# The first norm of a two-block kernel: the roots spread ahead of the last transposes and read in PSUM, the first scaled tile by itself, the first value products begun on the high part

## The chip, the cores and the metric

The kernel runs on one core of one Trainium2 chip. The core has TensorE (PE, matmuls; its weight loads are listed as PEld), VectorE (DVE), ScalarE (ACT), GpSimd (POOL) and SyncE (SP), which issues most DMAs. Each engine works through its own instructions in order and meets the others at semaphores. The metric is the device time of one launch in microseconds, as the median of several runs; lower is better.

## The reference

Two blocks, one after the other, on 512 tokens with 16 meta tokens ahead of them and a width of 1,024, all in fp32. The first block:

```python
h = jnp.concatenate([meta, x], axis=1)                 # 528 positions x 1024
z = rmsnorm(h, norm1_g[l])                             # h * rsqrt(mean(h*h) + EPS) * g
proj = z @ w_in[l]
q, fl, iv, og, pin, ga, gb = jnp.split(proj, SPLITS, axis=-1)
o_a = hgrn2_mixer(q, fl + b_f[l], iv, og, lb_all[l], head_norm_g[l])   # gated linear recurrence, 8 heads
o_b = pool_mixer(pin, w_pool[l], pool_scale[l])
mix = sigmoid(ga) * (o_a @ w_branch_a[l]) + sigmoid(gb) * (o_b @ w_branch_b[l])
h = h + mix @ w_out[l]
z = rmsnorm(h, norm2_g[l])
u, v = jnp.split(z @ w_up[l], 2, axis=-1)
h = h + (silu(causal_dwconv(u, conv_w[l], conv_b[l])) * v) @ w_down[l]
h = rmsnorm(h, final_norm_g)[:, N_META:]
```

The second block projects its norm again, runs two attentions (a latent one with rotary positions and one with forget gates), gates and mixes them, and adds a normed residual. `lb_all` is a softmax over the rows of `lb_logits`; `iv` are the values of the recurrence. Only the head of the first block, up to the first products of `z @ w_in`, is touched here.

## The kernel before

**Products in three terms.** Features lie on the 128 partitions, positions along the free dimension. The state hT is 8 tiles of 128 features x 528 positions; so is z. Each fp32 factor is split into a high part of the faster type fp32r and a rest of the same type: zhi, zlo for the activations, whi, wlo for the weights. A product is the sum of zhi x whi, zlo x whi and zhi x wlo, so a tile of 128 outputs over 8 tiles of features is 8 x 3 matmuls on each of two halves of 264 positions, 48 in all (line 841 is all of them). ScalarE writes the high parts (a copy that rounds), VectorE the low parts (a subtraction). This holds for weights too: a unit of weights (256 columns over 8 feature tiles, 128 x 2048) lands in one of three buffers, ScalarE writes whi (`w_high`), VectorE wlo (`w_low`), and TensorE waits for the latter. The first two units hold the value columns, 4 feature tiles each, so they are half as large.

**Accumulators.** PSUM is 8 banks of 512 fp32 columns. Products accumulate in slots of two banks; slot 0 is banks 0 and 1, slot 1 banks 2 and 3, slot 2 banks 4 and 5. A plan written ahead of the program gives each output tile its slot. The value tiles ("v", 0) and ("v", 1) have slots 0 and 1, computed as a pair, feature tile by feature tile. All later tiles of this stretch alternate between slots 0 and 1. Semaphore `pe_mark` counts finished pieces, `acc_free` the slots that were read out.

**The head.** SP loads the meta tokens (xm) and x (xt) with tokens on the partitions. TensorE transposes them into PSUM, six of eight feature tiles as the token blocks land (banks 0 to 5), the last two after banks 6 and 7 are read out. These transposes are copied to hT: tiles 0 to 3 by VectorE (`h_out` there), 4 to 7 by ScalarE. ScalarE squares x as it lands, one sum a token, then takes logarithm and exponential: the roots, one a token (`rs_ready`). They must be spread over all partitions: VectorE multiplies the identity by them (diag), and TensorE multiplies a matrix of ones by diag, two matmuls of 264 columns into banks 0 and 1 (`rb_spread`); ScalarE copies them to rb in SBUF. Then VectorE writes zt = hT x gain x rb (`norm_zt`, line 1838), ScalarE zhi from it (`norm_hi`), VectorE zlo (`norm_lo`, line 1844); there are two zt buffers. Between these stand the first weight units' parts, in an order written out by hand, as is everything in this kernel: no scheduler decides.

**Behind the value products.** TensorE transposes the small parameter rows (`turn_rows`, in the middle of the value products) and the value tiles (`turn_values`, lines 906 and 908, into banks 5 and 4). The first transposes of value tile 0 wait for ScalarE's copy of it (E<-PS 128x528); then come the q products. On ScalarE, between the last zhi and that copy, stand the high part of unit 2 and a small exponential that waits for VectorE's operations on `lb_logits` (`lb_sub`); between the copies of value tiles 0 and 1 stands the high part of unit 3.

## Time and profile before

| | us |
|---|---|
| three runs | 1569.93, 1570.18, 1575.18 |
| median | 1570.18 |
| profiled execution | 1573.95 |
| its span, first to last instruction | 1572.2 |
| TensorE busy | 1534.9 (98%) |
| VectorE busy | 839.7 (53%) |
| ScalarE busy | 694.7 (44%) |
| DMA, mean | 80 GB/s |

The rows further down come from the one profiled execution. A timeline row gives start and duration of a run of like instructions (x4: four of them), and in brackets the idle time before it and who ended it. A wait is put down to the last releaser. Matmul times are modelled at their ends, so spacing is read from windows: busy time over count. PEclk, the granted share of TensorE's clock, is 1.00 for 2.4 GHz and 0.50 for 1.2 GHz.

### The profile page before, as it was taken

The page shows a single profiled execution, that of the slowest core. Times are in us where ns is not written, and L with a number is a line of the kernel's source. Part 1 is how long each engine was busy: PE and PEld are TensorE (multiplying, and loading weights), DVE is VectorE, ACT ScalarE, POOL GpSimd, SP SyncE. Part 2 cuts the span into 40 slices and gives each one's busy share as a digit, 9 for nine tenths or more (in the row PEclk, how much of TensorE's full clock was granted, in tenths as well). Part 3 has the DMA queues.
Part 4 walks back from the last instruction along what each step waited for, and adds up shares of the span by engine and source line. Part 5 has one row for each costly group of instructions (what it writes and reads, how often), then busy time and mean ns, then how long its engine had stood idle before and what let it go on. Part 6 is the DMA issues. An engine that isn't in the chain of part 4 may idle for free.

```text
span 1572.2 us, 24005 instructions
## 1 busy us (share of the span) xinstructions
PE 1534.9 (98%) x10287; PEld 1350.5 (86%) x10287; DVE 839.7 (53%) x1234; ACT 694.7 (44%) x1036; POOL 3.6 (0%) x16
## 2 busy tenths in 40 slices
PE   7999999999999999999999899999999999999998
PEld 7999999999999989997888777778889877878888
DVE  6477766645645656563334676643233565653343
ACT  5565676654333223232233455542222666653232
POOL 0000000000000000000000000000000000000000
PEclk9999999999999999999999999999999999999999
DMA  6212111214323222232333300113232111122322
GB/s 228 81 55 88 54 55 56 67 31 147 108 81 97 91 92 97 84 105 75 100 94 101 54 1 28 55 54 107 80 108 81 55 54 55 54 68 81 107 81 81
DMA packets 130542, 125.46 MB, mean 80 GB/s; under 512 B 20170, under 2 KB 128485, under 8 KB 130053
## 3 DMA queue, kind: packets, MB, share of 16 engines
q1 hardware_dynamic: 129956, 120.36, 24.2%
q0 software_dynamic: 464, 3.56, 0.6%
q8 instruction: 82, 1.34, 0.4%
q14 instruction: 24, 0.19, 0.0%
q10 hardware_dynamic: 16, 0.00, 0.0%
HBM read 119.66 MB, written 4.26 MB: 79 GB/s over the span
## 4 chain that ended last, share of the span: by engine, by line
PE 89%; DVE 5%; ACT 3%; issue 2%; DMA 1%; DVEq 0%; SPq 0%; ACTq 0%
PE PS L841 75%; PE PS L953 3%; PE PS L1167 2%; PE PS L1110 2%; PE PS L1132 2%; DVE wlo L1798 1%; ACT whi L1307 1%; PE PS L1115 1%; PE PS L1116 1%; DMA raw<-in_w_out 0%; PE PS L1144 0%; PE PS L1117 0%; PE PS L965 0%; DMA xt<-in_x 0%; PE PS L1001 0%
## 5 line engine op out<-in xcount | busy, mean ns | idle before, releaser
L841 PE MATMUL PS<-zhi,whi 128*128 128x258 f32 (+2 forms) x1872 | 486.5, 320 | 6.6 <-DVE zlo L1844 3.3
L841 PE MATMUL PS<-zlo,whi 128*128 128x258 f32 (+2 forms) x1872 | 474.7, 313 | 0.0
L841 PE MATMUL PS<-zhi,wlo 128*128 128x258 f32 (+2 forms) x1872 | 474.4, 313 | 0.0
L841 PEld LDWEIGHTS PS<-zhi,whi 128*128 128x128 f32 x1872 | 308.5, 190 | 31.4 <-issue 9.3
L841 PEld LDWEIGHTS PS<-zhi,wlo 128*128 128x128 f32 x1872 | 307.2, 189 | 21.3
L841 PEld LDWEIGHTS PS<-zlo,whi 128*128 128x128 f32 x1872 | 307.3, 189 | 18.7
L1798 DVE TENSOR_TENSOR wlo<-raw,whi 128x2048 fp32r<-128x2048 f32 (+2 forms) x114 | 247.7, 2173 | 131.2 <-ACT whi L1307 131.1
L1307 ACT ACTIVATE whi<-raw 128x2048 fp32r<-128x2048 f32 (+2 forms) x114 | 207.3, 1819 | 155.6 <-DMA raw<-in_w_up 55.0
L1307 ACT ACTIVATE Pm<-PS,small 128x144 f32<-128x144 f32 (+3 forms) x128 | 68.7, 539 | 60.8 <-DVE small L2315 60.5
L2315 DVE TENSOR_REDUCE small<-PS 128x1 f32<-128x144 f32 (+3 forms) x128 | 63.3, 504 | 45.9 <-PE PS L1117 44.6
L841 PE MATMUL PS<-ghi,whi 128*128 128x512 f32 x176 | 70.3, 399 | 2.2 <-DVE glo L2210 2.2
L841 PE MATMUL PS<-ghi,wlo 128*128 128x512 f32 x176 | 70.2, 399 | 0.0
L841 PE MATMUL PS<-glo,whi 128*128 128x512 f32 x176 | 70.1, 398 | 0.0
L1307 ACT ACTIVATE nsq<-PS 128x512 f32<-128x512 f32 x32 | 19.1, 595 | 102.6 <-PE PS L841 101.2
L1307 ACT ACTIVATE E<-E 128x1056 f32<-128x1056 f32 (+2 forms) x32 | 33.6, 1049 | 52.5 <-DVE E L1942 33.7
L1132 PE MATMUL PS<-ident,Pm 128*128 128x128 f32 x320 | 53.7, 273 | 1.5 <-ACT Pm L1307 0.7
L953 PE MATMUL PS<-E 128*128 128x64 f32 (+1 forms) x448 | 51.8, 268 | 0.7 <-DVE E L1954 0.7
L1307 ACT ACT_TABLE_LOAD x37 | 47.5, 1283 | 7.7 <-PE PS L841 7.1
L841 PE MATMUL PS<-yhi,whi 128*128 128x512 f32 x128 | 50.5, 395 | 0.0
L841 PE MATMUL PS<-yhi,wlo 128*128 128x512 f32 x128 | 50.5, 394 | 0.0
L841 PE MATMUL PS<-ylo,whi 128*128 128x512 f32 x128 | 50.5, 394 | 0.0
L953 PEld LDWEIGHTS PS<-E 128*128 128x128 f32 (+1 forms) x448 | 48.8, 184 | 1.9 <-DVE E L1954 0.9
(351 smaller groups left out, 2150.7 us busy)
## 6 DMA issues: line engine op xcount, KB each, us to landing
raw<-in_w_in SPq DMA_DIRECT2D x50, 1024.0 KB, 5.1
raw<-in_w_up SPq DMA_DIRECT2D x22, 1024.0 KB, 5.1
raw<-in_w_out SPq DMA_DIRECT2D x8, 1024.0 KB, 5.2
raw<-in_w_down SPq DMA_DIRECT2D x8, 1024.0 KB, 5.1
raw<-in_w_br_mla SPq DMA_DIRECT2D x4, 1024.0 KB, 5.1
raw<-in_w_br_fox SPq DMA_DIRECT2D x4, 1024.0 KB, 5.0
raw<-in_w_down SPq DMA_DIRECT2D x4, 768.0 KB, 4.6
hspill<-hT SPq DMA_DIRECT2D x1, 2112.0 KB, 8.3
```

The lines of the kernel that those rows point to most:

```text
L841: ins = mm(o_, l_, r_, start=first, stop=last)
L953: ins = mm(PS[0:m, bank, 64 * it:64 * it + 64].rearrange("p (n b) -> p n b", b=half), e[:, hh, t0:t0 + m], rhs, start=True, stop=True)
L1110: mm(dst, qh[h % 2][:, t0:t0 + P], kh[h % 2][:, c0:c1], start=True, stop=True)
L1115: mm(dst, xqa[i_][:, t0:t0 + P], xka[i_][:, c0:c1], start=True, stop=False)
L1116: mm(dst, xqb[i_][:, t0:t0 + P], xkb[i_][:, c0:c1], start=False, stop=True)
L1132: ins = tr(PS[:, 2 + g % 2, P * x:P * (x + 1)], Pm[h % 2][:, o_:o_ + P], ident[:, :])
L1167: ins = mm(PS[64 * r:64 * r + 64, 7, q0:q0 + n], vtok[0:rows, j, v0:v0 + DV], PT[r][0:rows, c0:c0 + n], start=j == 0, stop=j == 4, skip_gr ...
L1307: return nc.scalar.activation(out_, in_, func, **kw)
L1798: V.tensor_tensor(lo[s_][:, 0:n_], raw[s_][:, 0:n_], hi[s_][:, 0:n_].bitcast(F32), ALU.subtract)\
L2315: V.tensor_reduce(negmax[:, s:s + 1], s_view(i), AX.XY if i == 3 else AX.X, ALU.max, negate=True).then_inc(A.m_ready, 1)
```

## The change

It does four things. (1) The roots' matmuls stand ahead of the last eight transposes, into banks 6 and 7, and the diagonal is built after one hT copy of VectorE's, not two; the last two feature tiles are transposed into banks 0 and 1. (2) No rb: VectorE reads the roots in PSUM when it scales (`root_gain`). (3) The first scaled tile is made by itself ahead of the first low weight part; the second low weight part stands one tile later; ScalarE copies hT tiles 2 and 3, ahead of its first high weight part, and VectorE only tiles 0 and 1. (4) In the value products the two terms with zhi come first, then the one with zlo, each with its own wait (`values_pair`). Since banks 0 and 1 are in use, the value tiles are in slots 1 and 2, and the first value transposes wait for both tiles to be copied.

```diff
--- before.py
+++ after.py
@@ -175,7 +175,7 @@
     for i in range(2):
         u = pl.unit([("w_in", i * D // 2, A_V, 256, 0)], KT // 2, 256)
         for m in range(2):
-            pl.piece(("v", m), u, 128 * m, KT // 2, "z", slot=m, k0=i * KT // 2, first=i == 0, last=i == 1)
+            pl.piece(("v", m), u, 128 * m, KT // 2, "z", slot=m + 1, k0=i * KT // 2, first=i == 0, last=i == 1)
     n = 2
     pair("q", A_Q, 0)
     pair("f", A_F, 0)
...
@@ -783,6 +782,18 @@
                 for ins in ends:
                     ins.then_inc(pe_mark, 1)
 
+            def values_pair(k0):
+
+                parts = [gemm_steps(("v", m)) for m in range(2)]
+                for k in range(KT // 2):
+                    pe.wait_ge(norm1.zhi_ready, k0 + k + 1)
+                    for step in parts:
+                        step(k, ((0, 0), (1, 0)), (0, 1))
+                    pe.wait_ge(norm1.z_ready, k0 + k + 1)
+                    ends = [step(k, ((0, 1),), (0, 1)) for step in parts]
+                for ins in ends:
+                    ins.then_inc(pe_mark, 1)
+
             def gemm(name, x_wait=None):
 
                 step = gemm_steps(name)
@@ -807,10 +818,10 @@
                 W = [t[:, 0:kt * cols].rearrange("p (k c) -> p k c", k=kt)
                      for t in (hi[s], lo[s])]
 
-                def step(k):
-                    for w, x in ((0, 0), (0, 1), (1, 0)):
+                def step(k, terms=((0, 0), (0, 1), (1, 0)), end=(1, 0)):
+                    for w, x in terms:
                         first = p.first and k == 0 and w == 0 and x == 0
-                        last = p.last and k == p.kt - 1 and w == 1
+                        last = p.last and k == p.kt - 1 and (w, x) == end
                         if p.mode == "values":
                             rows = KEYS[p.k0]
                             lhs = (ckhi, cklo)[x][:, P * p.k0:P * p.k0 + rows]
@@ -878,24 +889,23 @@
                         ins.then_inc(x_turned, 1)
             pe.wait_ge(h_copied, 1)
             pe.wait_ge(g1_copied, 1)
+            pe.wait_ge(diag_ready, 2)
+            for b in range(2):
+                ins = mm(PS[:, 6 + b, 0:HALF], ones[:, :], diag[:, HALF * b:HALF * (b + 1)], start=True, stop=True)
+            ins.then_inc(rb_spread, 1)
             for k in range(KT - 2, KT):
+                pe.wait_ge(h_copied, k - KT + 4)
                 for i in range(QB):
-                    ins = tr(PS[:, k, P * i:P * (i + 1)], xt[:, i, P * k:P * (k + 1)], ident[:, :])
+                    ins = tr(PS[:, k - KT + 2, P * i:P * (i + 1)], xt[:, i, P * k:P * (k + 1)], ident[:, :])
                 ins.then_inc(x_turned, 1)
-
-            pe.wait_ge(diag_ready, 2)
-            pe.wait_ge(h_copied, 3)
-            for b in range(2):
-                ins = mm(PS[:, b, 0:HALF], ones[:, :], diag[:, HALF * b:HALF * (b + 1)], start=True, stop=True)
-            ins.then_inc(rb_spread, 1)
-            pe.wait_ge(h_copied, KT // 2 + 1)
+            pe.wait_ge(h_act, 4)
 
...
@@ -1008,14 +1018,16 @@
                 if n[0] == "pool":
                     pe.wait_ge(pd_ready, n[1] + 1)
                 if n == ("v", 0):
-                    gemm_pair([("v", 0), ("v", 1)], norm1.z_ready)
+                    values_pair(0)
                     turn_rows()
-                    gemm_pair([("v", 0), ("v", 1)], norm1.z_ready, KT // 2)
+                    values_pair(KT // 2)
                     pe.wait_ge(prm_copied, 1)
                 elif n != ("v", 1):
                     gemm(n)
                 if pending is not None:
                     j = pending
+                    if j == 0:
+                        tile_freed(pe, ("v", 1))
                     turn_values(v_rows(j), j, v_turned, v_copied, ("v", j), (0, NM))
                     pending = None
                 if n[0] == "v":
@@ -1356,7 +1368,7 @@
 
             def h_out(k):
                 act.wait_ge(x_turned, k + 2)
-                A_(hT[:, k, NM:T], PS[:, k, :], ACT.Copy).then_inc(h_act, 1)
+                A_(hT[:, k, NM:T], PS[:, k if k < KT - 2 else k - KT + 2, :], ACT.Copy).then_inc(h_act, 1)
 
             nc.scalar.dma_start(*row_load(*ROW_LOADS[0])).then_inc(g1_in, 16)
             log_exp()
@@ -1370,17 +1382,18 @@
             tick(A_(xss, xss, ACT.Ln, scale=1.0 / D, bias=epst))
             settle()
             A_(xss, xss, ACT.Exp, scale=-0.5).then_inc(rs_ready, 1)
+            h_out(2)
+            h_out(3)
             w_high(0)
             h_out(4)
+            norm_hi(norm1, 0)
             h_out(5)
-            act.wait_ge(rb_spread, 1)
-            A_(halves(rb[:, :]), PS[:, 0:2, 0:HALF], ACT.Copy).then_inc(norm1.rb_ready, 1)
-            norm_hi(norm1, 0)
+            norm_hi(norm1, 1)
             h_out(6)
-            norm_hi(norm1, 1)
             h_out(7)
+            norm_hi(norm1, 2)
             w_high(1)
-            for k in range(2, KT):
+            for k in range(3, KT):
                 norm_hi(norm1, k)
             w_high(2)
             act.wait_ge(lb_sub, 1)
@@ -1822,15 +1835,17 @@
                 V.tensor_copy(hT[:, k, NM:T], PS[:, k, :]).then_inc(h_copied, 1)
 
             h_out(0)
-            h_out(1)
             dve.wait_ge(rs_ready, 1)
             dve.wait_ge(const_ready, 8)
             V.tensor_scalar(diag[:, 0:NM], ident[:, 0:NM], xss[:, QB:QB + 1], None, ALU.mult).then_inc(diag_ready, 1)
             V.tensor_tensor(diag[:, NM:T].rearrange("p (i c) -> p i c", i=QB),
                             ident[:, :].unsqueeze(1).broadcast_to([P, QB, P]),
                             xss[:, 0:QB].unsqueeze(2).broadcast_to([P, QB, P]), ALU.mult).then_inc(diag_ready, 1)
-            h_out(2)
-            h_out(3)
+            h_out(1)
+
+            def root_gain(k):
+                V.scalar_tensor_tensor(out=halves(zt[k % 2][:, :]), in0=halves(hT[:, k, :]), scalar=col("norm1", k),
+                                       in1=PS[:, 6:8, 0:HALF], op0=ALU.mult, op1=ALU.mult).then_inc(norm1.zt_ready, 1)
 
             def norm_zt(n, k):
                 if k == 0:
@@ -1852,25 +1867,25 @@
                     if k >= 1:
                         norm_lo(n, k - 1)
 
+            dve.wait_ge(h_copied, 3)
+            dve.wait_ge(g1_copied, 1)
+            dve.wait_ge(rb_spread, 1)
+            root_gain(0)
             w_low(0)
-            dve.wait_ge(h_copied, KT // 2 + 1)
-            dve.wait_ge(g1_copied, 1)
-            for k in range(KT + 1):
+            for k in range(1, KT + 1):
                 if k < KT:
                     if k >= 2:
                         dve.wait_ge(norm1.z_ready, k - 1)
-                    if k >= KT // 2:
-                        dve.wait_ge(h_act, k - KT // 2 + 1)
-                    norm_zt(norm1, k)
-                if k >= 1:
-                    norm_lo(norm1, k - 1)
-                if k == 2:
+                        dve.wait_ge(h_act, k - 1)
+                    root_gain(k)
+                norm_lo(norm1, k - 1)
+                if k == 3:
                     w_low(1)
...
```

On TensorE, from the transposes of token block 3 to the first products, before:

```order
L876 MATMUL PS<-ident,xt 128x128 [waits xt_in3]
L876 MATMUL PS<-ident,xt 128x128 x5
L883 MATMUL PS<-ident,xt 128x128 [waits g1_copied,h_copied]
L883 MATMUL PS<-ident,xt 128x128 x7
L889 MATMUL PS<-diag,ones 128x264 [waits h_copied,diag_ready]
L889 MATMUL PS<-diag,ones 128x264
L841 MATMUL PS<-zhi,whi_51 128x264 [waits w_lo,n1_z,h_copied]
L841 MATMUL PS<-zhi,whi_51 128x264
L841 MATMUL PS<-zlo,whi_51 128x264 x2
L841 MATMUL PS<-zhi,wlo_50 128x264 x2
```

and of the change:

```order
L887 MATMUL PS<-ident,xt 128x128 [waits xt_in3]
L887 MATMUL PS<-ident,xt 128x128 x5
L894 MATMUL PS<-diag,ones 128x264 [waits diag_ready,g1_copied,h_copied]
L894 MATMUL PS<-diag,ones 128x264
L899 MATMUL PS<-ident,xt 128x128 [waits h_copied]
L899 MATMUL PS<-ident,xt 128x128 x3
L899 MATMUL PS<-ident,xt 128x128 [waits h_copied]
L899 MATMUL PS<-ident,xt 128x128 x3
L852 MATMUL PS<-zhi,whi_51 128x264 [waits w_lo,n1_zhi,h_act]
L852 MATMUL PS<-zhi,whi_51 128x264
L852 MATMUL PS<-zhi,wlo_50 128x264 x2
```

The two spreading matmuls have moved ahead of eight transposes, and the first product waits for the high part of z (n1_zhi), no longer for the low one (n1_z).

On VectorE, from the first hT copy to the second low weight part, before:

```order
L1822 COPY hT_68<-PS 128x512 [waits x_turned] x2
L1828 TENSOR_SCALAR diag_96<-ident_59,small_64 128x16 [waits const_ready,rs_ready]
L1829 TENSOR_TENSOR diag_96<-ident_59,small_64 128x512
L1822 COPY hT_68<-PS 128x512 [waits x_turned] x2
L1798 TENSOR_TENSOR wlo0_50<-raw0_49,whi0_51 128x1024 [waits w_hi]
L1838 SCALAR_TENSOR_TENSOR zt0_76<-hT_68,prm_58,rb_78 128x528 [waits n1_rb,g1_copied,h_copied]
L1838 SCALAR_TENSOR_TENSOR zt1_77<-hT_68,prm_58,rb_78 128x528
L1844 TENSOR_TENSOR zlo_72<-zt0_76,zhi_71 128x528 [waits n1_zhi]
L1838 SCALAR_TENSOR_TENSOR zt0_76<-hT_68,prm_58,rb_78 128x528 [waits n1_z]
L1844 TENSOR_TENSOR zlo_72<-zt1_77,zhi_71 128x528 [waits n1_zhi]
L1798 TENSOR_TENSOR wlo1_53<-raw1_52,whi1_54 128x1024 [waits w_hi]
```

and of the change:

```order
L1835 COPY hT_68<-PS 128x512 [waits x_turned]
L1840 TENSOR_SCALAR diag_95<-ident_59,small_64 128x16 [waits const_ready,rs_ready]
L1841 TENSOR_TENSOR diag_95<-ident_59,small_64 128x512
L1835 COPY hT_68<-PS 128x512 [waits x_turned]
L1847 SCALAR_TENSOR_TENSOR zt0_76<-hT_68,prm_58,PS 128x528 [waits rb_spread,g1_copied,h_copied]
L1811 TENSOR_TENSOR wlo0_50<-raw0_49,whi0_51 128x1024 [waits w_hi]
L1847 SCALAR_TENSOR_TENSOR zt1_77<-hT_68,prm_58,PS 128x528
L1859 TENSOR_TENSOR zlo_72<-zt0_76,zhi_71 128x528 [waits n1_zhi]
L1847 SCALAR_TENSOR_TENSOR zt0_76<-hT_68,prm_58,PS 128x528 [waits h_act,n1_z]
L1859 TENSOR_TENSOR zlo_72<-zt1_77,zhi_71 128x528 [waits n1_zhi]
L1847 SCALAR_TENSOR_TENSOR zt1_77<-hT_68,prm_58,PS 128x528 [waits h_act,n1_z]
L1859 TENSOR_TENSOR zlo_72<-zt0_76,zhi_71 128x528 [waits n1_zhi]
```

Two hT copies are gone from VectorE, the first zt stands ahead of the first low weight part (wlo0), and the second (wlo1) follows one tile later than before, behind the last row shown.

On TensorE at the end of the value products, where the first value tile (E) is transposed, before:

```order
L841 MATMUL PS<-zlo,whi_54 128x264 x2
L841 MATMUL PS<-zhi,wlo_53 128x264 x2
L906 MATMUL PS<-ident,E_87 16x128 [waits acc_free0,prm_copied]
L908 MATMUL PS<-ident,E_87 128x128 x4
L841 MATMUL PS<-zhi,whi_57 128x258 [waits acc_free0,w_lo]
L841 MATMUL PS<-zhi,whi_57 128x258
```

and of the change:

```order
L852 MATMUL PS<-zlo,whi_54 128x264 [waits n1_z]
L852 MATMUL PS<-zlo,whi_54 128x264 x3
L916 MATMUL PS<-ident,E_86 16x128 [waits acc_free1,acc_free2,prm_copied]
L918 MATMUL PS<-ident,E_86 128x128 x4
L852 MATMUL PS<-zhi,whi_57 128x258 [waits w_lo]
L852 MATMUL PS<-zhi,whi_57 128x258
```

The transposes wait for the read-out of slots 1 and 2, which hold value tiles 0 and 1; before, they waited for slot 0, value tile 0. ScalarE's order there is the same in both kernels.

## Rows read from the trace of the kernel before

**Rows 1.** The page, busy time and its share of the span by engine.

```profile
PE 1534.9 (98%) x10287; PEld 1350.5 (86%) x10287; DVE 839.7 (53%) x1234; ACT 694.7 (44%) x1036; POOL 3.6 (0%) x16
```

**Rows 2.** Waits of TensorE, whole span: engine, line, releaser: total, times, longest, in us.

```profile
PE PS L841 <- DVE zlo L1844: 3.3, 1, 3.3
...
PE PS L841 <- DVE tmp L2149: 2.3, 1, 2.3
...
PE PS L841 <- DVE glo L2210: 2.2, 1, 2.2
...
PE PS L906 <- ACT E L1307: 0.8, 1, 0.8
```

**Rows 3.** Busy time by engine in windows of the head; PEclk is the granted clock.

```profile
core 0: us, PE busy (x) PEld busy (x) DVE busy (x) ACT busy (x) POOL busy (x), PEclk, DMA share, GB/s
...
12.57:14.10 1.53, 1.53 (x9) 1.05 (x7) 1.53 (x4) 0.91 (x2) 0.00 (x0) 1.00 1.08 329
...
17.45:22.86 5.41, 5.41 (x24) 5.41 (x25) 5.05 (x7) 3.19 (x6) 0.00 (x0) 0.50 0.00 0
22.86:31.97 9.11, 9.11 (x75) 8.90 (x74) 7.94 (x16) 3.97 (x6) 0.00 (x0) 1.00 0.57 204
```

**Rows 4.** Timeline of the head: start us, duration us, engine, line, operation.

```profile
11.03 0.54 ACT L1307 ACTIVATE small<-small 128x5 f32<-128x5 f32 x2
...
12.19 0.68 DVE L1829 TENSOR_TENSOR diag<-ident,small 128x512 f32<-128x512 f32 x1
12.42 1.06 ACT L1307 ACTIVATE hT<-PS 128x512 f32<-128x512 f32 x2
...
13.04 1.06 PE L889 MATMUL PS<-diag,ones 128*128 128x264 f32 x4
13.99 1.21 DVE L1798 TENSOR_TENSOR wlo<-raw,whi 128x1024 fp32r<-128x1024 f32 x1
14.14 0.61 ACT L1307 ACTIVATE rb<-PS 128x528 f32<-128x528 f32 x1 [0.65 <-PE PS L889]
15.12 1.44 DVE L1838 SCALAR_TENSOR_TENSOR zt<-hT,prm,rb 128x528 f32<-128x528 f32 x2
...
19.04 1.22 DVE L1798 TENSOR_TENSOR wlo<-raw,whi 128x1024 fp32r<-128x1024 f32 x1 [0.32 <-ACT whi L1307]
```

**Rows 5.** Timeline from the last scaled tiles to the second value copy.

```profile
25.87 0.77 DVE L1838 SCALAR_TENSOR_TENSOR zt<-hT,prm,rb 128x528 f32<-128x528 f32 x1
...
26.67 0.65 ACT L1307 ACTIVATE zhi<-zt 128x528 fp32r<-128x528 f32 x1 [0.78 <-DVE zt L1838]
...
29.25 2.29 DVE L1798 TENSOR_TENSOR wlo<-raw,whi 128x2048 fp32r<-128x2048 f32 x1 [0.87 <-ACT whi L1307]
...
31.93 0.21 ACT L1307 ACTIVATE small<-small 128x16 f32<-128x16 f32 x1 [2.81 <-DVE small L1882]
...
32.05 0.59 ACT L1307 ACTIVATE E<-PS 128x528 f32<-128x528 f32 x1
...
32.54 1.91 ACT L1307 ACTIVATE whi<-raw 128x2048 fp32r<-128x2048 f32 x1
...
32.79 0.27 PE L906 MATMUL PS<-ident,E 128*16 128x128 f32 x1 [0.82 <-ACT E L1307]
...
34.35 0.60 ACT L1307 ACTIVATE E<-PS 128x528 f32<-128x528 f32 x1
```

**Rows 6.** VectorE groups by shape: count, busy us, mean ns, idle before.

```profile
L2404 DVE SCALAR_TENSOR_TENSOR qh<-PS,trig 128x512 f32<-128x512 f32 x16 | 11.0, 686 | 5.6 <-PE PS L841 5.4
...
L1838 DVE SCALAR_TENSOR_TENSOR zt<-hT,prm,rb 128x528 f32<-128x528 f32 x8 | 6.0, 765 | 0.2
...
L2034 DVE SCALAR_TENSOR_TENSOR oblo<-PS,prm,obhi 128x516 fp32r<-128x516 f32 x4 | 3.0, 754 | 6.0 <-ACT obhi L1307 6.0
```

**Rows 7.** Windows right after two later idle stretches of TensorE (419.68 to 421.93, 722.73 to 724.96).

```profile
421.93:425.60 3.67, 3.67 (x18) 3.67 (x19) 2.47 (x4) 3.17 (x3) 0.00 (x0) 0.55 0.58 205
...
724.96:729.40 4.44, 4.44 (x13) 3.49 (x14) 2.49 (x3) 2.00 (x2) 0.50 (x1) 0.62 0.40 140
```

More of the change, by code:

```diff
@@ L327, in build_program @@
         zt[1], e = at("zt1", [P, T], F32, e)
-        rb, e = at("rb", [P, T], F32, e)
         cstage, e = at("cstage", [P, P + HEADS + MASKC], F32, e)
@@ L532, in build_program @@
         h_src = lambda k: hT[:, k, :]
-        norm1 = Norm("n1", h_src, KT, T, D, None, zt, rb, "norm1", zpair)
+        norm1 = Norm("n1", h_src, KT, T, D, None, zt, None, "norm1", zpair)
         norm2 = Norm("n2", h_src, KT, T, D, nsq, nzt, nrb, "norm2", zpair)
@@ L880, in _ @@
             pe.wait_ge(g1_copied, 1)
+            pe.wait_ge(diag_ready, 2)
+            for b in range(2):
+                ins = mm(PS[:, 6 + b, 0:HALF], ones[:, :], diag[:, HALF * b:HALF * (b + 1)], start=True, stop=True)
+            ins.then_inc(rb_spread, 1)
             for k in range(KT - 2, KT):
+                pe.wait_ge(h_copied, k - KT + 4)
                 for i in range(QB):
-                    ins = tr(PS[:, k, P * i:P * (i + 1)], xt[:, i, P * k:P * (k + 1)], ident[:, :])
+                    ins = tr(PS[:, k - KT + 2, P * i:P * (i + 1)], xt[:, i, P * k:P * (k + 1)], ident[:, :])
                 ins.then_inc(x_turned, 1)
-            pe.wait_ge(diag_ready, 2)
-            pe.wait_ge(h_copied, 3)
-            for b in range(2):
-                ins = mm(PS[:, b, 0:HALF], ones[:, :], diag[:, HALF * b:HALF * (b + 1)], start=True, stop=True)
-            ins.then_inc(rb_spread, 1)
-            pe.wait_ge(h_copied, KT // 2 + 1)
+            pe.wait_ge(h_act, 4)
             def turn_rows():
-                pe.wait_ge(h_act, KT // 2)
+                pe.wait_ge(h_act, KT - 2)
                 pe.wait_ge(prm_in, PRM_DMAS)
-                tr(PS[:, 4, 0:NROW1], prow[0:NROW1, 0, :], ident[0:NROW1, 0:NROW1])
-                tr(PS[:, 4, P:P + NROW2], prow[0:NROW2, 1, :], ident[0:NROW2, 0:NROW2]).then_inc(prm_turned, 1)
+                tr(PS[:, 0, 0:NROW1], prow[0:NROW1, 0, :], ident[0:NROW1, 0:NROW1])
+                tr(PS[:, 0, P:P + NROW2], prow[0:NROW2, 1, :], ident[0:NROW2, 0:NROW2]).then_inc(prm_turned, 1)
             def turn_values(src, j, turned, copied, tile_name, tiles):
@@ L922, in rec_step @@
                         else:
-                            pe.wait_ge(norm1.rb_ready, 1)
+                            pe.wait_ge(norm1.zt_ready, KT)
                         for c in range(4):
@@ L1871, in _ @@
             dve.wait_ge(prm_turned, 2)
-            tick(V.tensor_copy(prm[:, KT:NROW1], PS[:, 4, KT:NROW1]))
-            V.tensor_copy(prm[:, P:P + NROW2], PS[:, 4, P:P + NROW2]).then_inc(prm_copied, 1)
+            tick(V.tensor_copy(prm[:, KT:NROW1], PS[:, 0, KT:NROW1]))
+            V.tensor_copy(prm[:, P:P + NROW2], PS[:, 0, P:P + NROW2]).then_inc(prm_copied, 1)
             settle()
```

## The prediction

> **What bounds the kernel now.** Start with the busy shares of the page: TensorE 98% of the span, VectorE 53%, ScalarE 44% [rows 1]. The kernel is a chain of matmuls, so an edit at its head is worth exactly what it moves the moment at which TensorE gets into its unbroken stretch. Next, the list of TensorE's waits shows how little there is to take: the longest is 3.3 us, before the first value product, for the first low part zlo, and the wait for ScalarE's copy of a value tile (line 906) is 0.8 us [rows 2]. Then the windows around them. The products begin at 17.45 us and run at a granted clock of 0.50 (1.2 GHz) until 22.86: 24 matmuls in 5.41 us, 0.225 us each. From there to 31.97 it is 1.00 (2.4 GHz): 75 in 9.11 us, 0.121 us each. Then 0.82 us of nothing ahead of the transposes at 32.79, and the q products follow [rows 3, 5]. So the question is not when the value products start or end, but when TensorE gets past what stands behind them.
>
> That is answered by the two timeline stretches [rows 4, 5]. Read the second one backwards from 32.79, the transposes of value tile 0. They wait for ScalarE's copy of that tile (32.05 to 32.64). The value products had ended only at 31.97, but ScalarE was itself held until 31.93 by its small exponential, which waits for VectorE's three bound operations; these stand behind the third low weight part (29.25 to 31.54), that behind ScalarE's high part, which VectorE awaits until 29.25, that behind the last zhi (26.67), that behind the last zt (25.87 to 26.64). I call this the split chain. It and the products arrive within 0.1 us of each other. A shorter way into the products alone can thus gain next to nothing: what moves the end is the split chain, and what TensorE waits for behind it.
>
> **The head, part by part.** (a) The root's diagonal is built after one hT copy instead of two. The roots are there when ScalarE's pair ends, 11.03 + 0.54 = 11.57; after the small diagonal operation (0.15 at most) the large one starts at 11.76 rather than 12.19, and with its 0.68 ends at 12.45. The two spreading matmuls (four records, 1.06 us) now run ahead of the last eight transposes: 12.57 to 13.63 instead of 13.04 to 14.10 [rows 4]. (b) ScalarE's copy of the roots to rb, 0.61 us, goes; it ended at 14.75, under the first low weight part that VectorE was at until 15.12, so it priced nothing; (c) the first scaled tile no longer stands behind the first low weight part. It starts at 13.65, after the second hT copy (over by 13.1), against 15.12. (d) ScalarE takes over two hT copies (0.53 each) ahead of w_high(0): 11.5 to 12.55, then the high part of half size (half of the 1.91 us of a full one [rows 5], 1.0), over at 13.6, ready before VectorE wants it at 14.35. (e) From the first tile to the eighth VectorE has the same work as before: a tile (zt and zlo) costs (25.87 - 20.18) / 4 = 1.42 us, with 20.18 for the end of the second weight part's 1.14; a weight part costs 15.12 - 13.99 = 1.13. Six tiles, one more zt of 0.7 and two weight parts are 8.5 + 0.7 + 2.3 = 11.5 us [rows 4, 5]. Before, it started at 13.99 and met one stall of 0.32 us ahead of its second weight part, so that the eighth zt came at 25.87. Now it starts at 13.65, and the weight part stands one tile later, at 19.75, when ScalarE has its high part ready (three hT copies, three zhi and the part from 14.46 come to about 19.5). Eighth zt: 13.65 + 11.5 = 25.15, 0.7 us earlier.
>
> (f) The scaled tile reads the roots in PSUM. The nearest rows: zt from SBUF 765 ns for 528 columns; the same operation with an operand in PSUM 754 ns for 516 and 686 ns for 512 columns [rows 6]. I take no difference; the bound is 0.08 us either way on eight tiles, 0.6 us.
>
> (g) The value products begin on zhi and the low weight part: VectorE has the latter at 14.35 + 1.2 = 15.55, and the fourth ScalarE copy of hT, which the new banks need, ends at 15.6. They start at about 15.75, 1.7 us earlier. If the clock is at 0.50 until 22.9 again, 7.1 us hold 32 matmuls, the other 64 take 7.8 us, and they end at about 30.7; if it stays at 1.00 they are bound by the split chain (last zlo over at 27.3) and end near 28. The same 96 matmuls are issued. The loads of SP that wait for the products are issued earlier, never later, so no queue is moved behind anything new.
>
> The trace says that transposes can raise the clock: the spreading matmuls run at 1.00 [rows 3] though TensorE had run transposes alone since 7.4 us. The Trainium skill, "TensorE: Matmul & The Clock Gate", Part 4, PE-mode transpose, says the opposite, that transposes don't count as TensorE being busy in the same way; no trace here agrees. By the page the eight transposes moved between roots and products would not keep the clock up and the products would end late (30.7), by the row they might, and end near 28. The sum below is the same for both; the gap that follows is shorter by the page.
>
> **What stands behind.** The value tiles move from accumulator slots 0 and 1 to slots 1 and 2. Slot 2 is banks 4 and 5, into which the value transposes write. So the first transposes, which waited for the copy of value tile 0, now wait for the copy of tile 1 too. On ScalarE the order around it is unchanged: copy of tile 0, a whole high weight part, copy of tile 1. In the trace these start at 32.05, 32.54 and 34.35, and the last ends at 34.95 [rows 5]. Behind the waiting transposes on TensorE stands everything: the q products first, then f and all that follows, and with them the loads of SP that wait for their ends. With the split chain 0.7 us earlier, tile 1 is copied at 34.95 - 0.7 = 34.25, and with the 0.15 us between a copy and its transposes TensorE goes on at 34.4, where before it went on at 32.79: **1.6 us later**. The whole gain of the head is inside this wait, since the products are over at 30.7 at the latest: TensorE idles 3.7 to 6.4 us.
>
> **The clock.** After idle stretches of 2.3 and 2.2 us the rows show the clock at 0.55 and 0.62 for the following 3.7 and 4.4 us [rows 2, 7]; after the 3.3 us before the first products it was 0.50 for 5.41 us [rows 2, 3]. The new gap is longer than all of them. Each microsecond at 0.50 loses half: 3.67 x 0.45 / 0.5 = 3.3 us at half cost 1.65, and 5.41 cost 2.7. I take the middle, **2.1 us**; the 2.7 of before fall away, but inside the wait, so they pay nothing. The old wait of 0.8 is in the 1.6 already.
>
> **Sum.** 1.6 + 2.1 = 3.7 us slower. Against the profiled execution (span 1572.2, 1573.95 with what lies around it) that is 1577.7; that execution lies 3.8 above the median of the runs, 1570.18, so the forecast for the median is 1570.2 + 3.7 = **1573.9 us**, +0.24%. Nothing further back moves: the waits after this stretch are for work that itself follows TensorE. About 0.5%, 7.9 us, is what a measurement here can tell from no change, so this counts as no change.
>
> Bounds of the parts: the roots' matmuls could run at half clock (twice 1.06, so +0.8 after pipelining: 2.4 instead of 1.6), the PSUM operand gives 0.6 either way, the clock from 0 to 2.9: from +1.0 to +5.9.
>
> **Rivals.**
> A. The second copy is not late, because ScalarE's weight part does not stand ahead of it in time (it would have to be done early or to wait less). Then only the split chain counts: TensorE goes on at 32.64 - 0.7 + 0.15 = 32.1, 0.7 earlier: 1569.5. For it speaks only that the products end before either copy; against it that ScalarE's rows stand in this order in both kernels. 5%.
> B. The wait is as I say, but the clock is not dropped: +1.6, 1571.8. Against it are three drops after shorter gaps. 9%.
> C. Slower by over 0.5%: the place is the stretch of q and f products after the gap. If the clock comes back only late, each us at half costs 0.5, and with the 1.6 of the wait the limit of 7.9 is passed when it stays down for over 12.5 us after 34.4: 1578.1 and more. The longest half-clock stretch here under dense work is 5.41 us, so 5%; one more per cent for the same thing at a later gap.
> D. Faster by over 0.5%: the most the head could give is 1.7 of start, 2.7 of clock and 0.8 of wait, 5.2 us, under the limit. 1%.
> The forecast itself (wait and drop) has 79%.
>
> So 1573.9 with +1.0 to +5.9 is 1571.2 to 1576.1. The three runs before lie between 1569.93 and 1575.18, so a median carries a further microsecond or two, and the range goes to A on one side and to the edge of C on the other: 1570 to 1577.5. Chances: faster 0.01, same 0.93, slower 0.06.
>
> **What would show it.** In the new trace: the spreading matmuls at 12.6 us and the first zt near 13.65; zt still 0.77 us long; the first value product near 15.8; the last zhi near 25.9; TensorE's longest wait now at the first value transposes, 4 to 6 us, for ScalarE's copy of the second tile that starts just after a weight part; TensorE going on near 34.4; a half-clock stretch right behind. I am wrong if that wait is under 1 us, if the last zhi is not earlier, or if the clock after the gap is 1.00.

## The result, and the profile after

The changed kernel takes 1573.47 us (median of 20 runs); the kernel before took 1570.12 (20 runs), 3.35 us less. The ratio is 1.0018, interval [1.0012, 1.0024], which is 2.8 us: slower beyond the interval, and within the 0.5% that the prediction called no change. The forecast was 1573.9. Three slow runs, one of the changed kernel (1678.66) and two of the kernel before (3821.78 here, 3007.42 in a later session), are left out of the ratios and of what is pooled below; the other 19 of the changed kernel lie between 1572.03 and 1576.62. The pooled medians are 1573.54 for the changed kernel (41 runs, these and the two controls below) and 1570.32 for the kernel before (100 runs, the three sessions of the experiments), 3.2 us apart.

The busy shares answer to [rows 1] and tell nothing new:

```profile
PE 1533.4 (97%) x10287; PEld 1348.1 (86%) x10287; DVE 838.8 (53%) x1232; ACT 696.2 (44%) x1037; POOL 3.6 (0%) x16
```

TensorE's waits, which answer to [rows 2]: line 916 is the first value transpose (906 before), line 852 all products (841 before).

```profile
PE PS L916 <- ACT E L1319: 5.2, 1, 5.2
...
PE PS L852 <- DVE tmp L2164: 2.3, 1, 2.3
PE PS L852 <- DVE glo L2225: 2.2, 1, 2.2
...
PE PS L852 <- ACT hT L1319: 1.4, 1, 1.4
...
PE PS L852 <- DVE zlo L1859: 0.6, 1, 0.6
```

The wait for the first low part (3.3 us) has become one of 1.4 us for a ScalarE copy of hT and one of 0.6 for a low part inside the products. The wait for the value copy has grown from 0.8 to 5.2 us. Of the later waits the two longest stand as they were (2.3 and 2.2 us). Two others, for `vtok` and `hT` of VectorE, are 0.6 and 0.4 us shorter in this trace; the former differs by as much between traces of one and the same kernel (2.2 in the control, 1.6 here).

The timeline of the head and of the value copies, which answers to [rows 4, 5]:

```profile
10.78 0.54 ACT L1319 ACTIVATE small<-small 128x5 f32<-128x5 f32 x2
...
12.33 1.13 PE L894 MATMUL PS<-diag,ones 128*128 128x264 f32 x4 [1.09 <-DVE diag L1841]
...
13.59 0.77 DVE L1847 SCALAR_TENSOR_TENSOR zt<-hT,prm,PS 128x528 f32<-128x528 f32 x1 [0.81 <-PE PS L894]
...
15.75 0.48 PE L852 MATMUL PS<-zhi,whi 128*128 128x264 f32 x2 [1.42 <-ACT hT L1319]
...
19.54 1.22 DVE L1811 TENSOR_TENSOR wlo<-raw,whi 128x1024 fp32r<-128x1024 f32 x1
...
22.11 0.75 PE L852 MATMUL PS<-zlo,whi 128*128 128x264 f32 x4 [0.60 <-DVE zlo L1859]
...
25.72 0.65 ACT L1319 ACTIVATE zhi<-zt 128x528 fp32r<-128x528 f32 x1 [0.77 <-DVE zt L1847]
...
28.21 0.65 PE L852 MATMUL PS<-zlo,whi 128*128 128x264 f32 x4
28.30 2.29 DVE L1811 TENSOR_TENSOR wlo<-raw,whi 128x2048 fp32r<-128x2048 f32 x1 [0.87 <-ACT whi L1319]
...
30.99 0.22 ACT L1319 ACTIVATE small<-small 128x16 f32<-128x16 f32 x1 [2.81 <-DVE small L1897]
31.11 0.59 ACT L1319 ACTIVATE E<-PS 128x528 f32<-128x528 f32 x1
...
31.60 1.90 ACT L1319 ACTIVATE whi<-raw 128x2048 fp32r<-128x2048 f32 x1
...
33.40 0.60 ACT L1319 ACTIVATE E<-PS 128x528 f32<-128x528 f32 x1
...
34.10 0.37 PE L916 MATMUL PS<-ident,E 128*16 128x128 f32 x1 [5.24 <-ACT E L1319]
```

Read it from the end. The transposes at 34.10 come 0.1 us after the end of the second E<-PS (33.40 + 0.60). That copy follows the weight part (31.60 to 33.50), which follows the first copy, which follows the exponential at 30.99. The last products were over at 28.86. The whole chain is the one of before, and about 0.9 us earlier, of which 0.25 is that this execution had its roots earlier (10.78 against 11.03).

The same stretch in windows, which answer to [rows 3, 7]:

```profile
core 0: us, PE busy (x) PEld busy (x) DVE busy (x) ACT busy (x) POOL busy (x), PEclk, DMA share, GB/s
...
15.75:28.86 13.11, 12.50 (x98) 12.00 (x98) 11.97 (x21) 8.03 (x11) 0.00 (x0) 1.00 0.35 126
28.86:34.10 5.24, 0.00 (x0) 0.03 (x1) 3.62 (x13) 3.10 (x5) 0.00 (x0) 0.72 0.93 323
34.10:37.90 3.80, 3.80 (x18) 3.80 (x19) 2.05 (x3) 1.20 (x1) 0.00 (x0) 0.50 0.77 260
37.90:42.17 4.27, 4.27 (x37) 4.25 (x36) 1.02 (x1) 0.00 (x0) 0.00 (x0) 0.99 0.00 0
```

The products ran at 1.00 throughout (98 records in 13.1 us, where they took 14.5 before). After the 5.24 us of nothing the clock is 0.50: 18 matmuls in 3.80 us, then 37 in 4.27. And the scaled tile, with its operand in PSUM, against 765 ns in [rows 6]:

```profile
L1847 DVE SCALAR_TENSOR_TENSOR zt<-hT,prm,PS 128x528 f32<-128x528 f32 x8 | 6.1, 763 | 1.0 <-PE PS L894 0.8
```

Single executions of one kernel here scatter by 5 to 7 us. Most of that goes with the clock: over the 100 runs of the kernel before, time and mean granted clock have a correlation of about -0.9. Traces of single executions are therefore compared below from one moment in each, the start of ScalarE's pair of root operations (11.03 in the trace before, 10.78 after), to the first matmul of the second value transposes (line 906, 916), the point at which the head is over. The kernel before has one trace only.

| from the roots to | before | after, three traces |
|---|---|---|
| first value product | 6.42 | 4.97, 4.97, 4.97 |
| first value transposes | 21.76 | 23.32, 23.31, 23.32 |
| second value transposes | 28.07 | 31.39, 31.33, 31.78 |

### The profile page after: what moved, and what is told of

Read it like the earlier page. It is cut to its first block, busy times and chain, and to the rows that moved or that the text cites. A ratio compares the mean times of both kernels' runs of the same rounds, so it can differ in the third digit from the quotient of the medians.

```text
span 1573.6 us, 24005 instructions
## 1 busy us (share of the span) xinstructions
PE 1533.4 (97%) x10287; PEld 1348.1 (86%) x10287; DVE 838.8 (53%) x1232; ACT 696.2 (44%) x1037; POOL 3.6 (0%) x16
## 4 chain that ended last, share of the span: by engine, by line
PE 89%; DVE 5%; ACT 3%; issue 2%; DMA 0%; SPq 0%; DVEq 0%; ACTq 0%
PE PS L852 75%; PE PS L963 3%; PE PS L1179 2%; PE PS L1122 2%; PE PS L1144 2%; DVE wlo L1811 1%; ACT whi L1319 1%; PE PS L1127 1%; PE PS L1128 1%; DVE small L2330 0%; DMA xt<-in_x 0%; PE PS L1156 0%; PE PS L1129 0%; PE PS L975 0%; PE PS L918 0%
```

## The experiments

Each was timed in five rounds beside the kernel before (medians of it in the three sessions: 1570.4, 1570.31, 1570.23).

**The control, twice.** The changed kernel unaltered.

> The changed kernel again, as the control beside the others. Theory (the wait of the value transposes for the second tile, then a stretch at half clock): about 3 us over the kernel before, 1573.5, TensorE going on at about 34.1 to 34.4 with the clock at 0.50 for some 3 to 5 us behind it. Rival (the loss came of the clock's chance in that one execution, not of the wait): within 1 us of the kernel before.

Measured: 1573.59 us, ratio 1.0018 [1.0007, 1.0029]; the wait 5.2 us again, the gap between the two value transposes 8.02 us (8.07 in the first trace, 6.31 before).

> The changed kernel a third time, to pool with the first two, since single executions of every kernel here scatter by 5 us with the granted clock. Theory: 1573.5.

Measured: 1573.70, 1.0019 [1.0010, 1.0028]. The loss is there three times over, and in a run with a mean clock of 0.997 too (1572.57), so the rival, chance of the clock in one execution, is out.

**The copies side by side.**

```diff
             A_(lbe, lbt, ACT.Exp).then_inc(lb_exp, 1)
+            for h in range(2):
+                tile_done(act, ("v", h))
+                tile_free(A_(halves(v_rows(h)), acc_full(("v", h)), ACT.Copy), ("v", h))
```

(and the copies left out where they stood, the first of them ahead of the weight part.)

> The changed kernel with ScalarE's copy of value tile 1 put straight behind that of tile 0, ahead of the high weight part of 1.9 us. Theory: the copies end at 31.7 and 32.2, TensorE goes on at 32.35 instead of 34.1, 1.75 us earlier; the gap from 28.9 is still 3.5 us, longer than three that were followed by half clock, so the half-clock stretch stays: 1571.7, 1.8 under the changed kernel. Rival 1 (only the length of the half-clock stretch matters): same as the changed kernel, 1573.5. Rival 2 (the shorter gap also saves the clock): 3.7 under it, 1569.8.

```profile
30.04 0.22 ACT L1319 ACTIVATE small<-small 128x16 f32<-128x16 f32 x1 [2.81 <-DVE small L1903]
30.16 1.09 ACT L1319 ACTIVATE E<-PS 128x528 f32<-128x528 f32 x2
...
31.35 0.27 PE L916 MATMUL PS<-ident,E 128*16 128x128 f32 x1 [3.44 <-ACT E L1319]
```

Both copies in 1.09 us, and TensorE goes on after a gap of 3.44 us instead of 5.24: from the roots to the first transposes 21.51 us, 1.8 less than in the changed kernel, as expected. The clock still falls (7.83 us between the value transposes, 1.5 over 6.31). Measured: 1572.81 us, 1.0012 [1.0002, 1.0021], 0.7 under the changed kernel, where 1.8 were expected, with an interval from 1.8 under to 0.5 over it (resampled medians, 12 runs against 41). The trace is as the theory has it; the medians alone show neither the size nor, beyond noise, the direction. More on this below.

**Both copies ahead of the exponential.** The same three lines, but above the wait for `lb_sub` and the exponential.

> The changed kernel with both value copies of ScalarE ahead of the small exponential that waits for VectorE. Theory: the copies follow the products (end 28.9) at once, 28.95 to 30.1, TensorE goes on at 30.2 and the q products at 30.8, just behind their low weight part (30.6). That is 3.9 us earlier than the changed kernel, the gap is 1.4 us and the clock stays at 1.00, another 1.9: 5.8 under the changed kernel, 1567.7, and 2.4 under the kernel before. Rival (what is gained at the head is given back further on, by a wait for work that does not follow TensorE): 1570 or more, with a wait of over 1 us between 31 and 100 us that the changed kernel does not have.

The end of the products (line 852), the copies, the transposes and the exponential:

```profile
27.93 0.65 PE L852 MATMUL PS<-zlo,whi 128*128 128x264 f32 x4
...
28.38 1.11 ACT L1319 ACTIVATE E<-PS 128x528 f32<-128x528 f32 x2 [0.53 <-PE PS L852]
...
29.59 0.27 PE L916 MATMUL PS<-ident,E 128*16 128x128 f32 x1 [1.01 <-ACT E L1319]
...
30.66 0.22 ACT L1319 ACTIVATE small<-small 128x16 f32<-128x16 f32 x1 [1.17 <-DVE small L1903]
```

The gap is 1.01 us, TensorE goes on 19.13 us after the roots (23.32 in the changed kernel: 4.2 less), and the second transposes come at 25.74 instead of 31.4: 5.6 less, the wait and the clock together. Measured: 1569.59, ratio 0.9994 [0.9983, 1.0005]. Again:

> The repaired changed kernel again. The first time it came 4.0 us under the changed kernel where 5.8 were expected: the 3.9 of the wait, but not the 1.9 of the clock. Theory (the price of the clock was hidden by chance): pooled 5 us or more under the changed kernel. Rival (what the clock gives back here is lost at later gaps, whichever they are): pooled 4 us under it again.

Measured: 1568.83, 0.9992 [0.9983, 1.0001]. Pooled over 23 runs 1569.15, so 4.4 under the changed kernel, with an interval of about 0.9 either way (resampled medians), and 1.2 under the kernel before (0.2 to 2.0). The rival, a gain given back in full further on (1570 or more), is out. Two copies moved on ScalarE turn the loss into a small gain, which settles where the loss was. This is the repaired kernel in what follows.

**The gap filled.** The changed kernel with needless matmuls ahead of the wait.

```diff
                     if j == 0:
+                        for f in range(40):
+                            mm(PS[:, f % 2, 0:HALF], zhi[:, 0, 0:P], zhi[:, 0, 0:HALF], start=True, stop=True)
                         tile_freed(pe, ("v", 1))
```

> The changed kernel with 40 needless matmuls of 264 columns on TensorE between the value products and the wait for the copies (their sum is overwritten by the q products). Theory: they take 40 x 0.12 = 4.9 us of the 5.2 us gap, TensorE goes on at 34.1 as before but at 1.00: 1.9 us under the changed kernel, 1571.6, which is the price of the clock alone. Rival (the half clock costs nothing because another engine sets the pace of the q products): same as the changed kernel, 1573.5. If the needless matmuls reach past the copies: up to 1 us more.

```profile
33.23 0.60 ACT L1321 ACTIVATE E<-PS 128x528 f32<-128x528 f32 x1
...
33.88 0.28 PE L916 MATMUL PS<-ident,E 128*16 128x128 f32 x1 [0.38 <-ACT E L1321]
```

In windows, the filled gap and what follows it up to the second value transposes:

```profile
28.70:33.88 5.18, 4.80 (x41) 4.60 (x39) 3.62 (x13) 3.05 (x5) 0.00 (x0) 1.00 0.94 325
33.88:40.20 6.32, 6.32 (x53) 6.30 (x54) 3.08 (x3) 1.25 (x1) 0.00 (x0) 1.00 0.47 160
```

TensorE goes on 23.27 us after the roots, as in the changed kernel (23.32), but at 1.00: 6.32 us between the value transposes against 8.07. That is the price of the clock by itself, 1.75 us in this pair of traces. Measured: 1572.53, 1.0013 [1.0004, 1.0021].

> The changed kernel with the 40 needless matmuls again. The first time it came 1.1 us under the changed kernel where 1.9 were expected. Theory (the drop costs 1.9 by the records): pooled 1.5 to 2 us under it. Rival (part of it is lost at later gaps): 1 us.

Measured: 1572.63, 1.0017 [1.0006, 1.0028]; 6.33 us between the value transposes, though in this trace they come 24.26 us after the roots, 0.9 later than in the changed kernel, since the roots' matmuls ran at half clock (2.10 us instead of 1.13). Pooled over 22 runs 1572.60, 0.9 under the changed kernel (0.1 to 1.6): about half of what the traces of the stretch say, and hardly clear of noise. The price of the clock is shown by the traces, not by the medians.

**The slots alone.** The kernel before with the value tiles in slots 1 and 2 and the wait for both copies (and the parameter rows turned into bank 0, the first products waiting for ScalarE's two hT copies).

```diff
-            pl.piece(("v", m), u, 128 * m, KT // 2, "z", slot=m, k0=i * KT // 2, first=i == 0, last=i == 1)
+            pl.piece(("v", m), u, 128 * m, KT // 2, "z", slot=m + 1, k0=i * KT // 2, first=i == 0, last=i == 1)
...
+                    if j == 0:
+                        tile_freed(pe, ("v", 1))
```

> The kernel before with one part of the change alone: the value tiles in slots 1 and 2, so that the first value transposes wait for ScalarE's copies of both. Theory: TensorE goes on at 34.95 + 0.15 = 35.1 instead of 32.79, 2.3 us later, and the gap of 3.1 us is followed by half clock, up to 1.9 more: 1572.7 without and 1574.6 with it. Rival (the slots are harmless by themselves and the loss comes of the new head): 1570.4, as before.

```profile
30.70 0.59 ACT L1310 ACTIVATE E<-PS 128x528 f32<-128x528 f32 x1
...
32.99 0.60 ACT L1310 ACTIVATE E<-PS 128x528 f32<-128x528 f32 x1
...
33.69 0.37 PE L907 MATMUL PS<-ident,E 128*16 128x128 f32 x1 [4.12 <-ACT E L1310]
```

The pattern of the changed kernel without its head: copy, weight part, copy, transposes, with a gap of 4.12 us. Measured: 1573.53, 1.0026 [1.0016, 1.0036]. This part alone costs about what the whole change does. The first transposes come 23.81 us after the roots, 2.05 later than before where 2.3 were expected; the changed kernel has them at 23.32, so its head is 0.5 earlier. After the gap the clock is 0.50 for 2.61 us only, and the second transposes come 31.31 us after the roots, with the new head at 31.4. The rival that the slots are harmless is out; the new head, under this wait, is worth nothing that can be measured.

**The order of the copies without the new head.** The kernel before with the copy of value tile 0 ahead of the exponential. The edit moves this copy alone (`for h in range(1)`), not both as the expectation says; the copy of tile 1 stays behind the weight part.

> The kernel before with ScalarE's two value copies ahead of the small exponential, nothing else. Theory: the products end at 31.97 and the copy of tile 0 started at 32.05, so there is nothing to take: within 0.3 us of 1570.4. Rival (the order of the copies is a gain by itself, and the repaired changed kernel owes its time to it and not to its head): 1 us or more under it.

```profile
27.99 2.29 DVE L1804 TENSOR_TENSOR wlo<-raw,whi 128x2048 fp32r<-128x2048 f32 x1 [0.86 <-ACT whi L1307]
...
29.10 0.61 ACT L1307 ACTIVATE E<-PS 128x528 f32<-128x528 f32 x1 [1.25 <-PE PS L841]
...
29.86 0.27 PE L906 MATMUL PS<-ident,E 128*16 128x128 f32 x1
```

Here the products ran at 1.00 for longer than in the first trace, so that they were over at about 29.0 and the copy could follow at 29.10. The premise of the expectation, that there is nothing to take, does not hold in this trace: TensorE goes on 20.06 us after the roots, not 21.76, and the second transposes come at 26.40 instead of 28.07. Measured: 1570.86, 1.0002 [0.9991, 1.0013]: no gain in the median, but with a mean clock of 0.9941 against 0.9961. One slope fitted to the 253 runs of the table below says that 0.001 of mean clock goes with 0.89 us; put to the same clock by it, this kernel is 1.3 us under the kernel before, and the repaired kernel 1.1 under it. That is an estimate, but it is enough to leave the rival standing: whether the 1.2 us by which the repaired kernel beats the kernel before come of its head or of the order of its copies is not shown.

**The old order of terms in the repaired kernel.**

> The repaired changed kernel (both copies ahead of the exponential) with the old order of terms: each tile's products wait for its low part. Theory: the first product starts at 16.9 instead of 15.8, but the pace is VectorE's up to the second low weight part; from the fourth tile's low part (22.1) there are then 60 matmuls at 0.122 instead of 52: the products end at 29.6 instead of 28.9, 0.8 us later, so 0.8 over the repaired kernel. Rival (the early start on the high part brings nothing, since low parts set the end): no difference.

```profile
11.50 2.10 PE L894 MATMUL PS<-diag,ones 128*128 128x264 f32 x4 [1.83 <-DVE diag L1847]
...
17.07 0.48 PE L852 MATMUL PS<-zhi,whi 128*128 128x264 f32 x2 [1.97 <-DVE zlo L1865]
...
30.00 1.34 ACT L1319 ACTIVATE E<-PS 128x528 f32<-128x528 f32 x2 [1.70 <-PE PS L852]
...
31.44 0.27 PE L916 MATMUL PS<-ident,E 128*16 128x128 f32 x1 [0.75 <-ACT E L1319]
```

Measured: 1569.73, 0.9995 [0.9985, 1.0004], 0.6 over the pooled repaired kernel, and the first product 7.12 us after the roots instead of 4.97. Of the 2.15 us by which the first product is later, 0.97 are the roots' matmuls at half clock (2.10 instead of 1.13), which leaves about the 1.1 expected. But in this trace the clock fell a second time, to 0.50 from 18.18 to 21.59 us, the products ended 2.6 us later than in the repaired kernel (20.74 against 18.12 after the roots) instead of 0.8, and the second transposes come 2.1 later. So neither the trace nor the median (interval of the 0.6: from 1.6 under to 2.0 over) tells what the order of terms is worth.

**Two more moves.** The repaired kernel with the high part of unit 2 in ScalarE's idle time behind the fourth zhi, and with the q products of tile 0 ahead of the first value transposes (only the first move is shown).

```diff
                 norm_hi(norm1, k)
-            w_high(2)
+                if k == 3:
+                    w_high(2)
```

> The repaired changed kernel with two more moves: the high part of weight unit 2 right after the fourth zhi, where ScalarE idles 1.6 us, and the q products of tile 0 ahead of the transposes of value tile 0 (those follow them). Theory: VectorE's low part of unit 2 ends at 29.4 instead of 30.6, the q products start there, and the copies are no longer waited for: idle 0.8 us instead of 1.1 to 1.3 in all: 0.3 to 0.5 us under the repaired kernel, within noise. Rival (a wait further on for the later value transposes or low weight parts): 1 us or more over it.

```profile
26.84 2.29 DVE L1821 TENSOR_TENSOR wlo<-raw,whi 128x2048 fp32r<-128x2048 f32 x1
...
28.02 1.11 ACT L1322 ACTIVATE E<-PS 128x528 f32<-128x528 f32 x2 [2.33 <-PE PS L852]
...
29.28 0.48 PE L852 MATMUL PS<-zhi,whi 128*128 128x258 f32 x2 [1.06 <-DVE wlo L1821]
```

VectorE's part now ends at 29.13 and the q products start there, after an idle 1.06 us; the copies are not waited for. Measured: 1568.62, 0.9990 [0.9980, 1.0000].

> The fastest kernel so far again, as the candidate that beats both: 1568.6, 1.7 under the kernel before. If its lead over the repaired kernel (1.0) was chance, it comes out at 1569.3 or more.

Measured: 1568.84, 0.9987 [0.9976, 0.9999]. Pooled over 22 runs 1568.68: it beats the changed kernel by 4.9 us and the kernel before by 1.6 (0.9 to 2.4). Its lead over the repaired kernel (0.5) is within the scatter.

The kernels side by side. The last column is the time at a granted clock of 0.50 between 50 and 1560 us in each trace of the kernel, that is, behind the head.

| kernel | runs | median us | clock, mean of the runs | us at 0.50 behind the head |
|---|---|---|---|---|
| before | 100 | 1570.32 | 0.9961 | 10.2 |
| changed | 41 | 1573.54 | 0.9957 | 10.2, 6.8, 3.4 |
| copies side by side | 12 | 1572.82 | 0.9947 | 13.7 |
| gap filled | 22 | 1572.60 | 0.9969 | 6.8, 6.8 |
| slots alone | 11 | 1573.53 | 0.9936 | 17.1 |
| before, copy of tile 0 ahead of the exponential | 11 | 1570.86 | 0.9941 | 13.7 |
| repaired: copies ahead of the exponential | 23 | 1569.15 | 0.9961 | 17.1, 17.1 |
| repaired, old order of terms | 11 | 1569.73 | 0.9959 | 10.2 |
| repaired, and q products first | 22 | 1568.68 | 0.9965 | 6.8, 10.2 |

## Why the prediction was right

**The head.** Spreading matmuls forecast for 12.57 and seen at 12.33, first scaled tile 13.65 and 13.59, first product 15.75 and 15.75, last zhi 25.95 and 25.72. This execution had its roots 0.25 early (10.78 instead of 11.03), so counted from the roots the matmuls and the last zhi came when they were forecast to, and the first scaled tile and the first product 0.2 us later; the latter waited for ScalarE's fourth hT copy, as the prediction said. The split chain is 0.7 us earlier, as said (26.67 - 11.03 = 15.64 before, 25.72 - 10.78 = 14.94 now), and the operand in PSUM costs nothing (763 against 765 ns).

**The wait.** Forecast: TensorE goes on 1.6 us later. From the roots: 23.32 - 21.76 = 1.56. Forecast gap 3.7 to 6.4, seen 5.24. The clock stayed up through the products, for which the prediction had their end near 28 and the gap at 6.4; they ended at 28.86. The last zlo was over at about 27.1, but that did not bound them, as the prediction had it: from 22.11 on TensorE ran without a stop at 1.00 and set the end itself. Since the transposes wait for ScalarE and not for the products, this changed nothing in the sum. That the slots do it was argued; the slots alone in the old kernel and the two repairs of ScalarE's order show it.

**The clock.** Forecast 2.1, bounds 0 to 2.9. In the stretch itself it is 8.07 - 6.31 = 1.76, and 1.71 and 2.15 in the other two traces of the same kernel. 1.56 + 1.76 = 3.32 is also what the last line of the table of landmarks gives, and the medians differ by 3.2. That the 2.7 us which the kernel before loses to half clock in its products pay nothing when they fall away was right too: its copy waited for the exponential, not for the products.

**What was slightly off.** The roots' matmuls were bounded at 0.8 us of loss if the clock were low there: in the second trace of the filled kernel they took 2.10 instead of 1.13 us, and its scaled tile came 1.0 later. The upper bound of the clock's term, 2.9, is 0.2 more than the rows give (5.41 us at half, 2.7); the largest price measured was 2.15. I had not listed the stall of 0.60 us at the fourth tile's low part, behind the second weight part: with TensorE at 1.00 the products catch up with VectorE. It costs nothing beneath the wait.

**What stays open.** Each experiment that takes clock or wait away gives, in the medians, about 1 us less than its traces show for the head: 0.7 of 2.05 (31.39 - 29.34), 0.9 of 1.75, 4.4 of 5.6. By the mean clock, the missing microsecond lies behind the head. The changed kernel has 6.8 us at 0.50 around its gap (3.80 of them busy), which make 0.0022 of the mean clock; filling the gap raises the mean by 0.0012 only, and the repaired kernel by 0.0004. By the fitted slope (0.89 us for 0.001) the repaired kernel is 3.8 us under the changed one at the same clock, and the 0.0022 would give 1.9 more, together 5.7 against the 5.6 of the traces; for the filled gap the same estimate gives 1.6 against 1.75, for the copies side by side (3.4 us at 0.50 there) 2.7 against 2.05. The traces agree in kind: the gap of 2.25 us near 422 us, ahead of the products on `mixhi`, was followed by 0.50 in both traces of the filled kernel and both of the repaired one, and by 1.00 in all three of the changed kernel. The repaired kernel has 17.1 us at 0.50 behind the head in each of its two traces (both among its slower runs), the changed kernel 3.4 to 10.2. So part of the clock won at the head is missing at later gaps of the same kernels; whether by chance or because of the head, no run tells.

## What to carry to other kernels

When a tile moves to another accumulator, list who else writes those banks and what must now be read out first: a wait that names one more buffer is as long as everything that its reader's engine does in between. Before shortening a head, follow the chain behind it to the first point where another engine's order decides; here two copies moved past one small wait were worth 4.4 us, and the new head nothing that could be measured as long as they stood where they did. A long gap on TensorE can cost twice, once as idle time and again as a stretch at half clock. And where a median moves by a microsecond, read the mean clock beside it: 0.001 of it goes with 0.9 us here.

## What the runs showed of the hardware

Each gap of TensorE of 3.3 to 5.2 us at the head, eight of them in seven traces, was followed by a granted clock of 0.50. Behind the value products, the price as the time between the two value transposes less 6.31:

| gap us | traces | busy at 0.50 after it, us | price us |
|---|---|---|---|
| 5.24 | changed, three | 3.8, 3.8, 4.8 | 1.76, 1.71, 2.15 |
| 4.12 | slots alone | 2.6 | 1.19 |
| 3.44 | copies side by side | 3.4 | 1.52 |

So the second half of the price was 1.2 to 2.2 us and did not follow the length of the gap. After the gap of 3.44 us the clock fell only when TensorE had been busy again for 1.22 us. With matmuls in the gap (4.80 us busy of 5.18) the clock stayed at 1.00. A shorter gap goes either way: the one of 2.25 us near 422 us, the same in all 14 traces to 0.1 us, was followed by 0.50 in nine of them and by 1.00 in five.

Eight transposes between the roots' matmuls and the first products, with 1.42 us of idle time behind them, left the clock at 1.00 through the products in all nine such traces, where the kernel before, with 3.35 us idle, began them at 0.50; with the old order of terms in the repaired kernel, and 1.97 us idle, it fell to 0.50 1.1 us into the products. This is the row's side of the question raised in the prediction: after transposes alone, and with them in between, the clock was up. The roots' own matmuls found it at 1.00 where TensorE had been idle for 0.70 to 1.52 us before them (1.13 us, nine traces of the new head), and at 0.50 where it had been idle for 1.84 and 1.83 us (2.10 us, the second trace of the filled kernel and the one with the old order of terms).
